# A chunked delta-rule scan on one core: 64x64 products spread over four parts of the matmul array, with new places for its steps

## The chip, the core and the metric

The kernel runs on one core of a Trainium2 chip. The core has TensorE (PE in the profile; PEld is its weight loading), VectorE (DVE), ScalarE (ACT), GpSimd (POOL) and SyncE (SP), each with an instruction stream of its own, held together by semaphores. Matmul results land in PSUM: 8 banks of 512 fp32 values for each of 128 partitions. The metric is the time of one execution on the device in microseconds.

## The reference

Two transformer blocks run one after the other, on 256 context rows and 256 image rows of width 1024. The first has two gated FFNs, window attention and a gated scan; the second has two layers, of which the first mixes latent attention with an RWKV-7 scan, and each ends in a mixture of experts. Everything is fp32. The change touches only the RWKV-7 scan: 8 heads of width 64, forward and backward, over context and then image rows:

```
def wkv7_scan(state0, r, w, k, v, a_vec, b_vec, reverse):
    def step(S, inp):
        r_t, w_t, k_t, v_t, a_t, b_t = inp
        sa = jnp.einsum('bhij,bhj->bhi', S, a_t)
        S = (S * w_t[:, :, None, :] + sa[..., None] * b_t[:, :, None, :]
             + v_t[..., None] * k_t[:, :, None, :])
        return S, jnp.einsum('bhij,bhj->bhi', S, r_t)
    s_fin, ys = lax.scan(step, state0, xs, reverse=reverse)
```

## The kernel before

Class `Rwkv` computes the scan in **units**. A unit is one chunk of 128 tokens (`step`, 4 of them), one direction `d` and one pair of heads `j`: 4 x 4 x 2 = 32 units. Within a unit the sequential recurrence becomes matrix work. Decay factors `EB` and `EI` (ACT, two exponentials of 128 columns) scale the inputs into `RA` and `KB` (DVE). The products of `KB` and `RA` are 64-row matmuls with 256 columns (keys `mm`), which DVE copies through a triangular mask into `MM` (`copy_predicated`, L173, 512 columns each). Then the unit needs the inverse of a unit triangular 128x128 matrix for each of two heads. It is built in levels (`LEVELS`, 64 down to 1, finest first): POOL cuts the level's masked part `ML` out of the compact copy `MC`; TensorE forms T = ML X (key `lev`), ACT copies it to `T1`, TensorE forms two products of `T1` and X (key `xx`: X and its transpose are both kept in `XX`), and DVE adds them to `XX`. There are four 64x64 blocks, two heads `hh` by two token halves `b`. A matmul whose inputs lie in partition half `b` and whose output goes to partition half `b` uses one quarter of the array: quarter (b, b). So before, the level products use two of the four quarters, (0, 0) and (1, 1). The last level joins the halves, in an off-diagonal quarter, two matmuls for each product; its second product is named by `rwXF` and `rwT` (or `nv`, which is `T1` of buffer set 3). Then come `wu0` (128 columns), `wu1` (inverse times `wu0`), `st` (state update) and `y` (output).

Each level has 12 matmuls of 64x64 (4 in `lev`, 8 in `xx`), the first level 4. An fp32 matmul stands as two MATMUL records in the trace. Buffer set 0 of the four sets is carved out of `rwa`, so its operands are all named `rwa`; for sets 1 to 3 the names are `rwXX`, `rwT`, `rwMM`, `rwWU` (this holds `MC` and `ML` first), `rwXF`, and so on.

The order of the instructions is made by `run`: time is cut into rounds, a new unit starts every `APART` = 5 rounds, and in each round every running unit, oldest first, issues what stands between two `yield`s of its generator (`unit_pe`, `unit_act`, `unit_dve`, `unit_pool`). Four or five units are in flight. A level's `lev` goes in one round and its `xx` in the next. So five rounds are one period, in which TensorE issues as much as one unit has. `Banks.take` gives PSUM banks in rotation, and the taker waits until the bank's last user is emptied (`free`). A unit takes 20 banks. At the ends of the scan other work lies beside it: `amid_pe` at the start, and `close_*` with `late_pe` from round 146.

## Time and profile before

| | us |
|---|---|
| median of 3 runs | 2538.71 |
| lowest, highest | 2531.82, 2540.67 |
| the profiled execution | 2542.52 |
| its span in the profile | 2540.7 |

The page counts TensorE as busy for 92% of the span, DVE for 69%, ACT for 41%, POOL for 13%. The span is one chain of stages: FFNs and mixers before about 1400 us, the RWKV-7 scan from about 1405 to 1757 us, then the experts, the second mixer and the second experts. In the scan almost no DMA runs. A record of a 64x64 matmul lasts some 0.22 us from its start to its modelled end, while the next one on the same quarter starts much earlier, so the busy share of TensorE says less than the distances between starts. In the timeline, "x8" merges eight records; the time shown runs from the first start to the last end.

### The profile page before, as it was taken

The page shows a single profiled execution, that of the slowest core. Times are in us where ns is not written, and L with a number is a line of the kernel's source. Part 1 is how long each engine was busy: PE and PEld are TensorE (multiplying, and loading weights), DVE is VectorE, ACT ScalarE, POOL GpSimd, SP SyncE. Part 2 cuts the span into 40 slices and gives each one's busy share as a digit, 9 for nine tenths or more (in the row PEclk, how much of TensorE's full clock was granted, in tenths as well). Part 3 has the DMA queues.
Part 4 walks back from the last instruction along what each step waited for, and adds up shares of the span by engine and source line. Part 5 has one row for each costly group of instructions (what it writes and reads, how often), then busy time and mean ns, then how long its engine had stood idle before and what let it go on. Part 6 is the DMA issues. An engine that isn't in the chain of part 4 may idle for free.

```text
span 2540.7 us, 38727 instructions
## 1 busy us (share of the span) xinstructions
PE 2341.8 (92%) x15014; PEld 1751.2 (69%) x15014; DVE 1744.4 (69%) x3348; ACT 1051.7 (41%) x2068; POOL 337.2 (13%) x534
## 2 busy tenths in 40 slices
PE   7999999799989799989999899989999998998997
PEld 3788887465788799944454677775676775667775
DVE  4875687677756687834758666665678885748995
ACT  4222212224231434423134344442477773446884
POOL 0111110010001011000200233331011210001210
PEclk9999999899999899989998999999899999999998
DMA  8566654242226478711111000000389982126995
GB/s 307 190 204 199 216 197 161 94 141 91 101 74 206 142 265 269 254 43 66 39 43 35 18 3 3 2 3 26 109 286 341 324 314 108 59 70 216 338 339 188
DMA packets 114919, 386.47 MB, mean 152 GB/s; under 512 B 20144, under 2 KB 22320, under 8 KB 114480
## 3 DMA queue, kind: packets, MB, share of 16 engines
q1 hardware_dynamic: 76496, 275.81, 31.2%
q0 software_dynamic: 34848, 95.47, 11.3%
q10 hardware_dynamic: 3392, 12.72, 1.3%
q8 instruction: 119, 1.95, 0.3%
q14 instruction: 64, 0.52, 0.1%
HBM read 389.16 MB, written 26.21 MB: 163 GB/s over the span
## 4 chain that ended last, share of the span: by engine, by line
PE 37%; DVE 13%; DMA 8%; ACT 5%; issue 3%; POOL 0%; DVEq 0%; ACTq 0%; SPq 0%; POOLq 0%
PE ps L144 35%; DMA RG<-in_w 5%; DVE moe0wl L153 2%; PE ps L147 2%; DVE moe1wl L153 2%; DMA AR<-in_a 2%; DVE rwMM L173 1%; DVE f2wl L153 1%; DVE acc L161 1%; ACT moe0wh L150 1%; DVE H L161 1%; ACT moe1wh L150 1%; DVE rwXF L153 1%; ACT rwWU L150 1%; DVE rwXX L153 0%
## 5 line engine op out<-in xcount | busy, mean ns | idle before, releaser
L144 PE MATMUL ps<-H,RG 128*128 128x256 f32 (+2 forms) x1088 | 359.4, 491 | 14.0 <-ACT H L150 14.0
L161 DVE SCALAR_TENSOR_TENSOR acc<-AR,cs,acc 128x512 f32<-128x512 f32 x420 | 295.5, 746 | 48.9 <-DMA AR<-in_a 46.7
L144 PEld LDWEIGHTS ps<-H,RG 128*128 128x128 f32 (+1 forms) x1088 | 206.1, 194 | 149.8 <-issue 132.5
L153 DVE TENSOR_TENSOR moe0wl<-RG,moe0wh 128x1024 fp32r<-128x1024 f32 x144 | 173.6, 1219 | 42.8 <-ACT moe0wh L150 33.1
L150 ACT ACTIVATE moe0wh<-RG 128x1024 fp32r<-128x1024 f32 x144 | 150.8, 1061 | 73.9 <-DMA RG<-in_w 44.5
L200 POOL DMA_DIRECT2D AR<-in_a x152 | 82.1, 540 | 698.8 <-DVE acc L161 512.5
L150 ACT ACTIVATE f1wh<-RG 128x1024 fp32r<-128x1024 f32 x66 | 69.7, 1060 | 230.0 <-PE ps L144 229.9
L153 DVE TENSOR_TENSOR moe1wl<-RG,moe1wh 128x1024 fp32r<-128x1024 f32 x120 | 144.2, 1219 | 23.9 <-ACT moe1wh L150 19.8
L144 PE MATMUL ps<-f1hh,f1wh 128*128 128x512 f32 x352 | 142.5, 405 | 4.8 <-DVE f1hl L153 4.8
L150 ACT ACTIVATE moe1wh<-RG 128x1024 fp32r<-128x1024 f32 x120 | 125.9, 1060 | 46.8 <-DMA RG<-in_w 28.4
L144 PE MATMUL ps<-f1hl,f1wh 128*128 128x512 f32 x352 | 140.8, 400 | 0.0
L144 PE MATMUL ps<-f1hh,f1wl 128*128 128x512 f32 x352 | 140.7, 400 | 0.0
L153 DVE TENSOR_TENSOR f1wl<-RG,f1wh 128x1024 fp32r<-128x1024 f32 x66 | 80.4, 1221 | 54.8 <-ACT f1wh L150 53.1
L144 PE MATMUL ps<-f2hh,f2wh 128*128 128x256 f32 x352 | 103.2, 293 | 9.7 <-DVE f2hl L153 5.0
L144 PE MATMUL ps<-f2hh,f2wl 128*128 128x256 f32 x352 | 101.5, 288 | 0.0
L144 PE MATMUL ps<-f2hl,f2wh 128*128 128x256 f32 x352 | 101.4, 288 | 0.0
L150 ACT ACTIVATE f2wh<-RG 128x1024 fp32r<-128x1024 f32 x66 | 68.5, 1055 | 47.9 <-PE ps L144 47.9
L144 PE MATMUL ps<-moe0wh,moe0xh 128*128 128x512 f32 x184 | 78.6, 427 | 9.4 <-DVE moe0wl L153 9.3
L153 DVE TENSOR_TENSOR rwXX<-rwXX,ps 128x256 f32<-128x256 f32 (+1 forms) x120 | 47.1, 393 | 58.1 <-PE ps L144 57.5
L144 PE MATMUL ps<-rwa 64*64 64x64 f32 (+3 forms) x1228 | 74.5, 236 | 12.1 <-DVE rwa L153 5.6
L153 DVE TENSOR_TENSOR f2wl<-RG,f2wh 128x1024 fp32r<-128x1024 f32 x66 | 80.3, 1219 | 7.8 <-ACT f2wh L150 7.7
L144 PEld LDWEIGHTS ps<-f1hh,f1wh 128*128 128x128 f32 x352 | 68.6, 195 | 20.4 <-DVE f1hl L153 6.2
(633 smaller groups left out, 5742.3 us busy)
## 6 DMA issues: line engine op xcount, KB each, us to landing
RG<-in_w SPq DMA_DIRECT2D x524, 512.0 KB
AR<-in_a POOLq DMA_DIRECT2D x152, 512.0 KB, 3.9
moe0back<-moe_outs ACTq DMA_DIRECT2D x4, 1024.0 KB, 8.0
CT<-in_consts ACTq DMA_DIRECT2D x1, 2562.0 KB, 14.9
X<-in_x ACTq DMA_DIRECT2D x1, 2048.0 KB, 11.5
moe_rows<-moe0ht POOLq DMA_DIRECT2D x4, 512.0 KB, 5.4
moe1back<-moe_outs ACTq DMA_DIRECT2D x2, 1024.0 KB, 5.8
X<-in_ctx ACTq DMA_DIRECT2D x1, 1024.0 KB, 5.8
```

The source lines that it names most:

```text
L144: return Silent() if self.e is None else self.e.matmul(out, lhs, rhs, start=start, stop=stop, skip_group_check=True)
L147: return Silent() if self.e is None else self.e.transpose(out, x, ident)
L150: return Silent() if self.e is None else self.e.activation(out, x, f, **k)
L153: return Silent() if self.e is None else self.e.tensor_tensor(out, a, b, op)
L161: return Silent() if self.e is None else self.e.scalar_tensor_tensor(out=out, in0=a, scalar=s, in1=b, op0=op0, op1=op1)
L173: return Silent() if self.e is None else self.e.copy_predicated(out, mask, data)
L200: return Silent() if self.e is None else self.e.dma_start(out, src)
```

## The change

- `Banks` can hand out a pair of neighbouring banks (`take_pair`), and all banks are one PSUM tensor, so that one instruction can read both. A taker of a pair waits for the last users of both banks.
- In a level the block of head `hh` is kept in the partition half `b ^ hh`. `lev` and the first part of `xx` now use all four quarters in rotation, one matmul each, into a pair of banks. The second part of `xx` (4 matmuls) stays in the two diagonal quarters.
- T1 is I + ML X: DVE adds the identity while it empties the pair (128 columns). The product with T1 then replaces the old sum, so nothing is added afterwards: DVE copies 64 columns of the result, ACT the other 192. At the last small level DVE copies 128 columns, and ACT writes `XF` in four copies of 64x64. At the first level ACT copies 128 columns in place of a DVE add, and POOL forms the two halves of 64 columns in place of a DVE add.
- The product `mm` comes in two halves, for `KB[0]` in round 2 and for `KB[1]` in round 3, each with a mask copy; the transposes `kbt` follow in round 4. `wu1` moves from round 18 to the last slot of round 19, `y` and `st` from round 19 to round 20. The output copy of `y` on DVE now comes a round after the state's update.
- A round has four slots, and each step names its round and slot through `clock`.
- The three small ACT instructions for the chunk's middle are taken out of the units; six of 16 columns before the scan (`middles_act`) replace them.
- POOL writes the identity into the first 128 columns of `MM` (a copy of 2 x 128 columns beside a memset of 2 x 384).
- A unit takes 34 banks: 13 pairs and 8 single ones. The number of matmuls in a unit stays the same (86, or 172 records).

The level part of the diff, cut to its core:

```diff
+    def take_pair(self, key):
+        self.n += self.n % len(self.tiles) == len(self.tiles) - 1
+        b = self.n % len(self.tiles)
+        self.n += 2
+        self.hold(key, [b, b + 1])
+        return self.tiles[b], self.tiles[b + 1]
...
-            for u in list(running):
-                if next(u, "over") == "over":
-                    running.remove(u)
+            for _ in range(self.SLOTS):
+                for u in list(running):
+                    if next(u, "over") == "over":
+                        running.remove(u)
...
+        yield from to(2, 2)
+        self.mm_pe(e, n, 0, KB, RA)
+        yield from to(3, 2)
+        self.mm_pe(e, n, 1, KB, RA)
+        yield from to(4, 2)
         ps = g.banks.take(("kbt", n))
...
+            r = 4 + 2 * i if i else 5
+            if i == 6:
+                yield from to(r, 0)
+                self.wu0_pe(e, n, RA, MM, state, v)
+            yield from to(r, 1)
             key = ("lev", n, i)
-            ps = g.banks.take(key)
+            ps = g.banks.take_pair(key) if li else g.banks.take(key)
...
+            if i == 0:
+                e.wait_ge(*S.pool.at(("x1", n, 0)))
+                for k, b in enumerate(both):
+                    for hh in range(2):
+                        ins = e.matmul(ps[1 - hh][both[k ^ hh], 0:64], XX[b, 2 + hh, :], self.IC[b, :], True, True)
+            elif li:
...
+                for k, b in enumerate(both):
+                    for hh in range(2):
+                        ins = e.matmul(ps[hh][both[k ^ hh], 0:64], ML[b, hh, :], XX[b, 1 - hh, :], True, True)
...
+                yield from to(r + 1, 1)
                 key = ("xx", n, i)
-                ps = g.banks.take(key)
+                ps = g.banks.take_pair(key) if li else g.banks.take(key)
...
                 if li:
...
+                    for k, b in enumerate(both):
+                        for hh in range(2):
+                            ins = e.matmul(ps[hh][both[k ^ hh], 0:64], XX[b, 2 + hh, :], T1[b, hh, :], True, True)
+                    ins.then_inc(*p.up(("x0", n, i)))
                     for hh in range(2):
                         for b in both:
-                            e.matmul(ps[b, 128 + hh * 64:192 + hh * 64], T1[b, hh, :], XX[b, 1, hh, :], True, True)
-                    for hh in range(2):
-                        for b in both:
-                            ins = e.matmul(ps[b, hh * 64:(hh + 1) * 64], XX[b, 1, hh, :], T1[b, hh, :], True, True)
+                            ins = e.matmul(other[b, 64 + 64 * hh:128 + 64 * hh], T1[b, hh, :], XX[b, 2 + hh, :], True, True)
...
+        yield from to(2, 1)
+        e.wait_ge(*S.act.at(("ei", n)))
+        e.tensor_tensor(KB[:, 0, :], self.BB[d][:, j, cc], EI[:, :], MUL).then_inc(*v.up(("kb", n, 0)))
...
+                e.tensor_tensor(T1[:, :, :], g.banks.pair(("lev", n, i))[:, :, 0:64], one, ADD).then_inc(*v.up(("t", n, i)))
...
+        yield from to(20, 0 if step < 3 else 3)
+        if step < 3:
...
+            yield from to(21, 0)
         y = self.YB[:, j, cc]
```

How the change moves instructions is best seen in the order on the engines. First, TensorE in the middle of a period, before: a level's `xx` of set 2, a `lev` of set 3, then the four products `mm` of the new unit (set 0) together, and its transposes right behind.

```order
L144 MATMUL ps6<-rwXX2,rwT12 64x64 [waits rw_act]
L144 MATMUL ps6<-rwXX2,rwT12 64x64 x3
L144 MATMUL ps6<-rwT12,rwXX2 64x64 x4
L144 MATMUL ps7<-rwXX3,rwWU3 64x64 [waits rw_pool,rw_dve]
L144 MATMUL ps7<-rwXX3,rwWU3 64x64 x3
L144 MATMUL ps0<-rwa 128x256 [waits rw_dve]
L144 MATMUL ps1<-rwa 128x256
L144 MATMUL ps0<-rwa 128x256
L144 MATMUL ps1<-rwa 128x256
L147 MATMUL ps2<-CT,rwa 128x128 x2
```

The same place in the changed kernel:

```order
L144 MATMUL ps<-rwXX2,rwWU2 64x64 [waits rw_act,rw_pool,rw_dve]
L144 MATMUL ps<-rwXX2,rwWU2 64x64 x3
L144 MATMUL ps<-nv,rwXX3 64x64 [waits rw_dve]
L144 MATMUL ps<-nv,rwXX3 64x64 x3
L144 MATMUL ps<-rwXX3,nv 64x64 x4
L144 MATMUL ps<-rwa 128x256 [waits rw_dve]
L144 MATMUL ps<-rwa 128x256
L144 MATMUL ps<-rwT12,rwXX2 64x64 x4
L144 MATMUL ps<-rwXX2,rwT12 64x64 x4
L144 MATMUL ps<-rwXX3,rwWU3 64x64 [waits rw_pool,rw_act]
L144 MATMUL ps<-rwXX3,rwWU3 64x64 x3
L144 MATMUL ps<-rwa 128x256 [waits rw_dve]
```

The products `mm` are now in two pieces with level products between them, and the first piece waits for DVE.

Second, TensorE where a unit ends (set 1) and the next one's levels begin, in the changed kernel: `y`'s last products, an `xx` of set 2, a `lev` of set 3, the first level of a younger unit (set 0), and `wu0` of set 2.

```order
L144 MATMUL ps<-rwMM1,rwvk 64x128 x2
L144 MATMUL ps<-rwMM1,rwWU1 64x128 x2
L144 MATMUL ps<-rwT12,rwXX2 64x64 [waits rw_dve]
L144 MATMUL ps<-rwT12,rwXX2 64x64 x3
L144 MATMUL ps<-rwXX2,rwT12 64x64 x4
L144 MATMUL ps<-rwXX3,rwWU3 64x64 [waits rw_pool,rw_act]
L144 MATMUL ps<-rwXX3,rwWU3 64x64 x3
L144 MATMUL ps<-rwa 64x64 [waits rw_pool,rw_dve]
L144 MATMUL ps<-rwa 64x64 x3
L144 MATMUL ps<-rwst,rwRA2 128x128
L144 MATMUL ps<-rwvk,rwMM2 128x64 x2
```

Before, this first level took a single bank. Now it takes a pair, and it waits for a count of DVE as well as for one of POOL. Its data come from POOL alone: the count is that of a bank's last user, which in the rotation is the `y` of the unit that ends here (the same in every period). Before, `wu1`, `st` and `y` stood at this place behind the transposes, and no level product waited for the output copy.

Third, VectorE at the same place. Before (the unit that ends is in set 3), from the mask copies on:

```order
L173 COPY_PREDICATED rwMM2<-CT,ps0 128x512 [waits rw_pool,rw_pe]
L173 COPY_PREDICATED rwMM2<-CT,ps1 128x512 [waits rw_pe]
L164 COPY rwk<-ps4 128x128 [waits rw_pe]
L153 TENSOR_TENSOR rwst<-rwst,ps3 64x64 x2
L158 TENSOR_SCALAR rwst<-rwst,rwEB3 128x128 [waits rw_dve]
L153 TENSOR_TENSOR rwXX1<-rwXX1,ps6 128x256 [waits rw_pe]
```

And in the changed kernel (the unit that ends is in set 1):

```order
L153 TENSOR_TENSOR rwst<-rwst,ps 64x64 [waits rw_pe]
L153 TENSOR_TENSOR rwst<-rwst,ps 64x64
L158 TENSOR_SCALAR rwst<-rwst,rwEB1 128x128 [waits rw_dve]
L164 COPY rwXX2<-ps 128x128 [waits rw_pe]
L153 TENSOR_TENSOR nv<-ps,rwa 128x128 [waits rw_pe]
L164 COPY rwk<-ps 128x128
```

The output copy (`rwk`) moved from ahead of the state's update to behind it, and behind the answers to the `xx` and the `lev` that TensorE issues after `y`.

## Rows read from the trace of the kernel before

**Rows 1.** The page, part 1: busy time, share of the span, instructions.

```profile
PE 2341.8 (92%) x15014; PEld 1751.2 (69%) x15014; DVE 1744.4 (69%) x3348; ACT 1051.7 (41%) x2068; POOL 337.2 (13%) x534
```

**Rows 2.** Busy times by stretch: length, then PE, PEld, DVE, ACT, POOL, clock, DMA.

```profile
1530.00:1585.00 55.00, 50.09 (x930) 42.24 (x924) 35.42 (x115) 22.26 (x91) 19.84 (x40) 1.00 0.01 2
```

**Rows 3.** Chain that ended last, 1568 to 1590: start, us, what; mask copies of successive units.

```profile
1568.25 1.34 DVE rwa L173 x2
...
1578.36 1.35 DVE rwMM L173 x2
...
1588.49 1.33 DVE rwMM L173 x2
```

**Rows 4.** Timeline of PE in one period: start, us, instruction, idle before.

```profile
1574.40 0.22 PE L144 MATMUL ps<-rwXF,rwT 64*64 64x64 f32 x1
1574.86 0.45 PE L144 MATMUL ps<-rwXX,rwWU 64*64 64x64 f32 x8 [0.24 <-DVE rwXX L153]
...
1576.33 0.45 PE L144 MATMUL ps<-rwXX,nv 64*64 64x64 f32 x8
1576.62 0.40 PE L144 MATMUL ps<-nv,rwXX 64*64 64x64 f32 x8
1576.85 0.40 PE L144 MATMUL ps<-rwa 64*64 64x64 f32 x8
1577.18 1.13 PE L144 MATMUL ps<-rwRA,rwXX 64*128 64x256 f32 x8
1578.24 0.44 PE L147 MATMUL ps<-CT,rwXX 128*128 128x128 f32 x2
...
1580.15 0.63 PE L144 MATMUL ps<-rwa 64*64 64x64 f32 x16
1581.01 0.45 PE L144 MATMUL ps<-rwXX,nv 64*64 64x64 f32 x8 [0.23 <-ACT nv L150]
...
1581.80 0.43 PE L144 MATMUL ps<-rwa,rwWU 64*64 64x64 f32 x8
1582.59 0.44 PE L144 MATMUL ps<-rwXX,rwMM 64*64 64x64 f32 x4 [0.36 <-DVE rwXF L153]
```

**Rows 5.** Timeline of PE: an off-diagonal product (rwXF) beside a diagonal one.

```profile
1644.95 0.23 PE L144 MATMUL ps<-rwXX,rwWU 64*64 64x64 f32 x2
1644.96 0.27 PE L144 MATMUL ps<-rwXF,rwT 64*64 64x64 f32 x1
1645.01 0.28 PE L144 MATMUL ps<-rwXX,rwWU 64*64 64x64 f32 x3
...
1645.13 0.22 PE L144 MATMUL ps<-rwXX,rwWU 64*64 64x64 f32 x1
1645.19 0.22 PE L144 MATMUL ps<-rwXF,rwT 64*64 64x64 f32 x1
```

**Rows 6.** Timeline of DVE in the same period.

```profile
1576.36 0.28 DVE L153 TENSOR_TENSOR rwRA<-abr,rwEB 128x128 f32<-128x128 f32 x1
1576.56 0.28 DVE L153 TENSOR_TENSOR rwXX<-rwbb,rwT 128x128 f32<-128x128 f32 x1
...
1577.29 0.41 DVE L153 TENSOR_TENSOR rwXX<-rwXX,ps 128x256 f32<-128x256 f32 x1
1578.34 1.36 DVE L173 COPY_PREDICATED rwMM<-CT,ps 128x512 f32<-128x512 uint32 x2 [0.64 <-PE ps L144]
...
1580.19 0.46 DVE L153 TENSOR_TENSOR rwst<-rwst,ps 64x64 f32<-64x64 f32 x2
```

**Rows 7.** Timeline of ACT in the same period.

```profile
1575.93 0.19 ACT L150 ACTIVATE rwEB<-H 128x1 f32<-128x1 f32 x1
...
1579.74 0.64 ACT L150 ACTIVATE rwWU<-rwMM 64x128 f32<-64x128 f32 x2 [2.17 <-DVE rwMM L173]
1580.40 0.38 ACT L150 ACTIVATE rwKBt<-ps 128x256 f32<-128x256 f32 x1
1580.68 0.27 ACT L150 ACTIVATE nv<-ps 128x128 f32<-128x128 f32 x1
```

More of the change, by code:

```diff
@@ L349, in __init__ @@
         self.CL, self.VL, self.ncst = CL, VL, ncst
-        self.banks = Banks([outer.enter_context(nc.psum_tensor(f"ps{i}", [P, 512], F32)) for i in range(8)])
+        self.banks = Banks(outer.enter_context(nc.psum_tensor("ps", [P, 8, 512], F32)))
         sb = self.sb
@@ L2668, in pool @@
             e.wait_ge(*o.now())
+        for d in range(2):
+            e.tensor_tensor(self.LC[d][:, 5, :], self.LC[d][:, 5, :], self.IC[:, :], ADD).then_inc(*o.up())
+            e.wait_ge(*o.now())
         for B in self.sets:
@@ L2692, in run, with clock, to @@
                 beside(e, r)
+    def clock(self):
+        at = [0]
+        def to(r, slot):
+            for _ in range(r * self.SLOTS + slot - at[0]):
+                at[0] += 1
+                yield
+        return to
     def last(self, j):
@@ L2787, in unit_pe @@
         src, dst = self.halves(d)
-        yield
-        yield
-        yield
-        got = []
-        for hh in range(2):
-            got.append(g.banks.take(("mm", n, hh)))
-            for tok in g.banks.free(("mm", n, hh)):
-                e.wait_ge(*tok)
-        e.wait_ge(*S.dve.at(("kb", n)))
-        for q in range(2):
-            for hh, b in enumerate(both):
-                ins = e.matmul(got[hh][:, q * 256:(q + 1) * 256], KB[b, q, :], RA[b, :], True, True)
-                if q:
-                    ins.then_inc(*p.up(("mm", n, hh)))
+        to = self.clock()
+        yield from to(2, 2)
[3 more added lines that the diff above has]
+        yield from to(4, 2)
         ps = g.banks.take(("kbt", n))
@@ L2836, in unit_pe @@
                 if li:
+                    other = ps[0]
+                    if li == 1:
+                        other, ps = g.banks.take(("xf", n)), ps[::-1]
+                        for tok in g.banks.free(("xf", n)):
+                            e.wait_ge(*tok)
+                    for k, b in enumerate(both):
+                        for hh in range(2):
+                            ins = e.matmul(ps[hh][both[k ^ hh], 0:64], XX[b, 2 + hh, :], T1[b, hh, :], True, True)
+                    ins.then_inc(*p.up(("x0", n, i)))
@@ L2845, in unit_pe @@
                         ins = e.matmul(ps[src, hh * 64:(hh + 1) * 64], T1[dst, hh, :], XF[dst, hh, dst], True, True)
[L2846 to L2847 removed]
+                ins.then_inc(*p.up(("x1", n, i)))
+        yield from to(19, 3)
         ps = g.banks.take(("wu1", n))
@@ L2855, in unit_pe @@
         ins.then_inc(*p.up(("wu1", n)))
-        yield
+        yield from to(20, 0)
         u = WU[:, 1, :]
-        e.wait_ge(*S.act.at(("wu1", n)))
+        out = g.banks.take(("y", n))
+        for tok in g.banks.free(("y", n)):
+            e.wait_ge(*tok)
+        e.matmul(out[:, 0:P], state, RA[:, P:2 * P], True, False)
         if step < 3:
@@ new lines, in unit_dve @@
+        yield from to(4, 0)
+        masks(1)
+        one = mid(self.IC[:, :], 2, 64)
+        for i, li in self.levels()[1:]:
+            if li:
+                yield from to(4 + 2 * i, 1)
+                e.wait_ge(*S.pe.at(("t", n, i)))
+                e.tensor_tensor(T1[:, :, :], g.banks.pair(("lev", n, i))[:, :, 0:64], one, ADD).then_inc(*v.up(("t", n, i)))
+                g.banks.done(("lev", n, i), v.now())
+                yield from to(5 + 2 * i, 1)
+                e.wait_ge(*S.pe.at(("x0", n, i)))
+                new = g.banks.pair(("xx", n, i))
+                if li > 1:
+                    e.tensor_copy(XX[:, 0, :], new[:, 1, 0:64]).then_inc(*v.up(("x0", n, i)))
+                    g.banks.done(("xx", n, i), v.now(), S.act.at(("x1", n, i)))
+                else:
+                    e.tensor_copy(XX[:, 0:2, :], new[:, :, 0:64]).then_inc(*v.up(("x0", n, i)))
+                    g.banks.done(("xx", n, i), v.now())
+            else:
+                yield from to(5 + 2 * i, 0)
+                e.wait_ge(*S.pe.at(("x1", n, i)))
+                e.tensor_copy(XF[src, :, dst], two(g.banks.of(("xx", n, i))[src, 0:128])).then_inc(*v.up(("xf", n)))
+                g.banks.done(("xx", n, i), v.now())
@@ new lines, in unit_dve @@
+        yield from to(20, 0 if step < 3 else 3)
+        if step < 3:
+            last = e0 + (P - 1 if d == 0 else 0)
+            e.wait_ge(*S.pe.at(("st", n)))
+            e.wait_ge(*S.pe.at(("y", n)))
+            e.wait_ge(*v.at(("ts", n)))
+            for lo in (0, 64):
+                q = slice(lo, lo + 64)
+                e.tensor_tensor(state[q, q], state[q, q], g.banks.of(("st", n))[q, lo:lo + 64], ADD).then_inc(*v.up())
+            g.banks.done(("st", n), v.now())
+            e.wait_ge(*v.now())
+            e.tensor_scalar(state, state, EB[:, last:last + 1], None, MUL).then_inc(*v.up())
+            v.note(("end", n))
+            yield from to(21, 0)
@@ L2997, in unit_dve @@
         g.banks.done(("y", n), v.now())
[L2998 to L3008 removed]
+        if step == 3:
+            v.note(("end", n))
     def unit_pool(self, e, n, step, d, j, B):
```

265 lines of the change are left out of this document (128 added, 137 removed).

## The prediction

> **What bounds the kernel now.** I read the page first: TensorE is busy for 92% of the span [rows 1]. Then the stretches: inside the scan TensorE works 50.1 of 55 us, DVE 35.4, ACT 22.3, POOL 19.8, at granted clock 1.00 and with a DMA share of 0.01 [rows 2]. So no transfer and no other engine fills the time. Then the chain of waits: the mask copies of successive units start at 1568.25, 1578.36 and 1588.49 [rows 3], a period of 10.12 us for each unit. 32 units start in the scan, so 31 periods lie between the first and the last.
>
> Then the timeline of TensorE in one period [rows 4], read by distances between starts. Eight records in the two diagonal quarters take 0.23 us: from 1576.62 to 1576.85. So a quarter takes a record each 0.058 us. A group that starts after idle time takes 0.05 more at its second record: four records in one quarter (1582.59, 0.44 long, of which 0.22 is the last record's own length) have starts 0.22 apart, 0.107 + 2 x 0.058. Where the tile shape changes, the distance to the next start is longer: the group at 1576.85 ends its starts at 1577.03, and 1577.18 comes 0.147 later instead of 0.058, so a change costs 0.09. The real waits are three in the period: 1580.57 (0.63 long from 1580.15, less 0.22) to 1581.01, beyond the pace 0.38; 1582.01 to 1582.59, 0.52; and 1574.40 to 1574.86, 0.40. Together 1.3 us. The rest, 8.8 us, is work at TensorE's pace.
>
> **What an answer costs** [rows 4, 6, 7]. DVE starts 0.26 us after the last start of a 64x64 group (1577.03 to 1577.29), and 0.41 after that of `mm` (1577.18 + 1.13, less the last record's 0.38, to 1578.34). TensorE starts 0.05 after the answering instruction ends (ACT 1580.68 + 0.27 = 1580.95, with rounding, to 1581.01). DVE instructions of 128 columns last 0.28 and start 0.20 apart (1576.36, 1576.56). A mask copy occupies 0.64 (1.36 for two, less 0.72). ACT: 128 columns 0.27, 256 columns 0.38.
>
> **Part one, the products.** The diagonal quarters bound the levels. Before, each of them has 2 matmuls at the first level and 6 at each of five levels: 32, of two records. Now it has 1 and 1 + 3 at each of five: 21. That removes 11 x 2 x 0.058 = 1.28 us for each unit, if the off-diagonal quarters run beside the diagonal ones. Rows 5 show three quarters at once: `rwXF` is an off-diagonal product; its four records (1644.96 to 1645.19) lie among eight diagonal ones (1644.95 to 1645.13), which keep their 0.18 from first to last start. Twelve records fit in 0.24 us, 0.022 each. The off-diagonal quarter there shares its inputs' half with one diagonal quarter and its outputs' half with the other. Four at once no row shows.
>
> `mm` in two pieces: one more change into and out of its shape, and one less between it and `kbt`: +0.09. A piece of two matmuls takes 0.32 (first records, with the start) + 0.30 to the next shape, twice: 1.25, where [rows 4] has 1577.18 to 1578.24, 1.06; in all +0.19. The work becomes about 8.8 - 1.28 + 0.19 = 7.7, and a little less where the first record's extra 0.05 goes: 7.55 in the walk below.
>
> **Part two, the waits.** I walk one period by the order and the prices above. A is the oldest unit in its levels, B and C are younger, N is the new one. Prices that no row has: DVE's copy of 64 columns, between 0.21 to 0.23 (two adds of 64x64 in 0.46) and 0.28: 0.22, occupying 0.17. ACT's copy of 192 columns, between 0.27 and 0.38: 0.33. ACT's 64x64 copies for `XF`, between 0.19 (one column) and 0.31: 0.22, and nothing waits for them soon. Zero is A's last level product.
> - B's `xx` runs beside it, 6 records to a diagonal quarter, last start 0.35. C's `lev` starts to 0.47. ACT answers in order: A's T1 at 0.48, `wu0` at 0.66, B's 192 columns from 0.83 to 1.16. A's `XF` product starts at 0.80 and B's `lev` at 1.21. The diagonal quarters stood idle for 0.68.
> - DVE has a queue here: C's T1 at 0.78, the two `RA`, `XF`, B's T1 at 1.59, C's copy at 1.79, and then `KB[0]` from 1.96 to 2.25. C's `xx` is issued from 1.38 to 1.67, and `mm` could start at 1.82, but waits for `KB[0]` to 2.30: 0.48.
> - From there TensorE never waits for long: B `xx` 2.94, C `lev` 3.34, second `mm` 3.55, B `lev` 4.18, C `xx` 4.35, transposes 4.79, `wu1` 5.28, the state products 5.72 (with 0.04 for `wu1`'s copy), `y` to 6.91, B `xx` 7.11, C `lev` 7.51. The mask copies (3.04 and 4.38 on DVE) cover nothing that TensorE needs sooner, since each answer has 0.8 us or more.
> - The first level of N could start at 7.63. It takes a bank that `y` held, and DVE's output copy stands behind C's T1: 7.57 + 0.26 = 7.83, copy from 8.04 to 8.33, TensorE at 8.38. Wait: 0.75.
> - `wu0` 8.64, the next last level 9.46.
>
> So the period is 9.46 us, with 1.9 us of waits where there were 1.3. The gain in work, 1.25, loses half to new waits: 0.66 us for each period.
>
> Of banks: a unit takes 34 where it took 20, so that eight are gone round in 2.2 us (9.46 x 8 / 34) instead of 4.0, and `y` holds one from 5.72 to 8.33. The Trainium skill says of this in "TensorEngine Tiling (Array Packing)", Gotcha 1: PSUM Pressure, that different row tiles have to write to different banks and so need more of them; my walk has it as the wait of 0.75, and without it the period would be 8.7.
>
> **Off the path.** POOL's memset and identity copy together cost between 0.95 (as now) and about 1.4; POOL would be busy for some 4 of 9.5 us, and each mask level is asked for a round earlier: nothing. DVE loses about 0.6 us in a period, ACT gains 1: both are under 7. Six ACT instructions of 16 columns before the scan, by the row of 0.19 [rows 7], cost at most 1.1 on the path and at least 0.5, as ACT starts overlap: 0.8. At the end of the scan five levels lose about 0.2 us each in latency, and `wu1` and `y` come a round or more later, in rounds that hold little; the closing of heads 2 now asks for an output of its own round, a stop of about 0.5. These cancel to within 1.5: zero.
>
> **The sum.** 31 x 0.66 = 20.5, less 0.8: 19.7 us. The profiled execution has 2542.52 (span 2540.7) and would come to 2522.8. It lies 3.8 above the median of the three timed runs, so that against the median the forecast is 2538.7 - 19.7 = **2519.0**.
>
> **The rivals.**
> 1. *The off-diagonal quarters do not run beside both diagonal ones, and it becomes slower.* Then a `lev` takes 0.23 and an `xx` 0.47 as now, 0.117 more in each of 11 groups, ten of them on the path, and the new waits stay: 9.46 + 1.17 = 10.63, or 31 x 0.51 + 0.8 = 16.6 more, 2555. It turns from gain to loss where more than 0.66 is lost, six of the groups. Against it: [rows 5] for three quarters. For it: no row for four.
> 2. *TensorE's issue is the limit, and nothing changes.* The longest dense stretch in rows, 8 records in 0.23, is 0.029 each, and only a stretch of twelve reaches 0.022 [rows 4, 5]; with 0.022 a `lev` takes 0.18 instead of 0.12 and the period is 9.8 (2530), with 0.029 it is rival 1. Halfway, at some 0.025, a `lev` takes 0.20 and an `xx` 0.40: 6 x 0.08 + 5 x 0.05 = 0.73, period 10.2, 2542. The Trainium skill has just such a rule in "TensorE: Matmul & The Clock Gate", section "Wait — 56ns, not 53.3ns?": starts never come closer than about 25 ns, however small the matmul. By that rule the result would be this rival's; pairs of starts 0.01 us apart in [rows 5] speak against it for different quarters.
> 3. *The waits come out smaller.* If the bank wait is hidden, 8.71 for the period: 2538.7 - 43.7 + 0.8 = 2496. Order and rotation speak against it, since the wait is there in each period. Without any wait (7.55) it would be 2460, which the answer times forbid.
> 4. *The waits grow instead*: DVE's queue before `KB[0]` holds seven instructions, and each 0.1 there moves the period by 0.1. At 10.0 the result is 2536, no change.
>
> **Chances.** Forecast (2507 to 2531): 0.52. Rival 3: 0.16. Rivals 2 and 4, no change: 0.19. Rival 1 and anything slower: 0.13. A measurement of this kernel can tell about 0.3%, 7.6 us, from no change. Faster by more: 0.52 x 0.96 + 0.16 = 0.66; within: 0.21; slower: 0.13. To leave out no more than 2 in 10 the range goes from 2496 (rival 3) to 2549, halfway into rival 1.
>
> **What would show it.** Mask copies of successive units 9.46 us apart, not 10.12. Eight records of a `lev` within some 0.12 to 0.18 us between first and last start; 0.23 would be rival 1. The first level waiting for DVE, some 0.7 us; the first piece of `mm` waiting for DVE's multiply, some 0.5; the `lev` after `rwXF` waiting for ACT. DVE busy a little less, ACT a little more in the scan, and every stage outside it as before. The prediction is wrong if periods are under 9 (waits overrated) or over 9.9 (products or queue underrated), or if another stage moves by more than 2 us.

## The result

The changed kernel takes 2569.27 us (median; 2554.74 to 2572.72), the kernel before beside it 2537.15 (2531.82 to 2540.67): a ratio of 1.0111, interval 1.0076 to 1.0145. It is 32 us slower by the medians, 28 by the ratio; the ratio rests on four executions of each kernel. The forecast was 2519.0, and 2569 is also outside its range. The profiled execution has 2572.72, its span 2570.9.

The page of the changed kernel, part 1, and the row of TensorE's granted clock from part 2:

```profile
PE 2337.3 (91%) x15014; PEld 1729.8 (67%) x15014; DVE 1726.1 (67%) x3380; ACT 1087.9 (42%) x2170; POOL 348.2 (14%) x600
...
PEclk9999999899999899999998989899999999998998
```

Against [rows 1] busy times hardly differ: 4.5 us less of PE, 18 less of DVE, 36 more of ACT. The row of the clock has an 8 in slices 24 and 26 (of 64.3 us each), which lie in the scan; before, no slice wholly within the scan has one. The windows say where to look. Length, then PE, PEld, DVE, ACT, POOL, granted clock, DMA share:

```profile
1530.00:1585.00 55.00, 45.04 (x826) 35.26 (x822) 28.77 (x107) 25.29 (x98) 18.61 (x44) 0.91 0.01 2
...
1640.00:1695.00 55.00, 46.38 (x768) 36.54 (x761) 26.68 (x97) 23.88 (x92) 17.75 (x42) 0.81 0.01 2
...
1582.00:1595.00 13.00, 10.12 (x226) 7.90 (x218) 7.95 (x31) 6.60 (x25) 4.75 (x11) 1.00 0.00 1
1570.00:1575.00 5.00, 4.60 (x63) 2.89 (x63) 3.08 (x12) 2.06 (x8) 1.15 (x3) 0.56 0.00 0
```

[Rows 2] had 930 PE records in 55 us at clock 1.00. Now there are 826 at 0.91, later 768 at 0.81. Two different things are in that: TensorE works 45 instead of 50 us of 55 (it stops more), and part of the time its clock is at the lower of its two levels, 1.2 GHz instead of 2.4. From 1570 to 1575 nearly all of the time is at it (0.56); from 1582 to 1595 none.

So the scan is read in two numbers for each kernel below: the period at full clock (the mean distance between first mask copies of successive units, over those periods of the fourth to the 27th that hold no slow clock), and how much of the time between the first unit's mask copy and the last's was at 1.2 GHz, summed over the clock's records in the trace. Before: period 10.11, none at 1.2 GHz, 318.7 us in all. Changed: period 10.40, 64.9 us at 1.2 GHz, 348.6 us. The 29.9 us between them are the loss; the stages before the scan start and end as before, those behind it only start later.

The 24 periods from the fourth to the 27th divide this loss. They take 242.8 us before and 269.7 in the changed kernel. Of the 26.9 between, 24 x (10.40 - 10.11) = 7 are the longer period at full clock. The other 20 go with the 51.2 us at 1.2 GHz that lie in these periods, 0.39 for each. The seven periods at the two ends hold the remaining 3. So most of the loss is the slow clock.

One period at full clock, TensorE. Start, us, instruction, idle before and what ended it:

```profile
1583.15 0.34 PE L144 MATMUL ps<-rwXX,rwWU 64*64 64x64 f32 x8
1583.28 0.33 PE L144 MATMUL ps<-nv,rwXX 64*64 64x64 f32 x8
1583.40 0.43 PE L144 MATMUL ps<-rwXX,nv 64*64 64x64 f32 x8
1584.47 0.70 PE L144 MATMUL ps<-rwa 64*128 64x256 f32 x4 [0.63 <-DVE rwa L153]
...
1589.15 0.39 PE L144 MATMUL ps<-rwMM,rwWU 128*64 128x128 f32 x4
1589.47 0.34 PE L144 MATMUL ps<-rwT,rwXX 64*64 64x64 f32 x8
...
1589.86 0.29 PE L144 MATMUL ps<-rwXX,rwWU 64*64 64x64 f32 x6
1591.34 0.34 PE L144 MATMUL ps<-rwa 64*64 64x64 f32 x8 [1.19 <-DVE rwk L153]
...
1592.95 0.32 PE L144 MATMUL ps<-rwa 64*64 64x64 f32 x4
1593.23 0.44 PE L144 MATMUL ps<-rwXF,rwT 64*64 64x64 f32 x4
1593.96 0.34 PE L144 MATMUL ps<-rwXX,rwWU 64*64 64x64 f32 x8 [0.28 <-POOL rwa L153]
```

Eight records of a `lev` or of the first part of `xx` last 0.34, less the last record's 0.22: 0.12 from first to last start, half of the 0.23 of [rows 4]. The four quarters run side by side in full. The three stops stand where the forecast has them, and each is longer: from 1583.61 (1583.40 + 0.43 - 0.22) to 1584.47, 0.86; from 1589.93 to 1591.34, 1.41; from 1593.05 to 1593.96, 0.91, in which only XF's product runs.

DVE in the longest of these stops (in every other `step` the output copy is an add, as here):

```profile
1589.65 0.47 DVE L153 TENSOR_TENSOR rwst<-rwst,ps 64x64 f32<-64x64 f32 x2 [1.86 <-PE ps L144]
1590.16 0.29 DVE L158 TENSOR_SCALAR rwst<-rwst,rwEB 128x128 f32<-128x128 f32 x1
1590.48 0.29 DVE L164 COPY rwXX<-ps 128x128 f32<-128x128 f32 x1
1590.68 0.28 DVE L153 TENSOR_TENSOR nv<-ps,rwa 128x128 f32<-128x128 f32 x1
1591.00 0.29 DVE L153 TENSOR_TENSOR rwk<-rwk,ps 128x128 f32<-128x128 f32 x1
```

The state's adds start at 1589.65, 0.11 after the modelled end of the last product of `y` (1589.15, 0.39 long), though their own product `st` came before `y`'s other products; DVE had been idle for 1.86 us. Behind them in the queue stand the scaling, the two answers, and the output copy (`rwk`), which ends at 1591.29. TensorE starts 0.05 later.

### The profile page after: what moved, and what is told of

It is laid out like the page before. It is cut to its first block, busy times and chain, and to the rows that moved or that the text cites. A ratio compares the mean times of both kernels' runs of the same rounds, so it can differ in the third digit from the quotient of the medians.

```text
span 2570.9 us, 38923 instructions
## 1 busy us (share of the span) xinstructions
PE 2337.3 (91%) x15014; PEld 1729.8 (67%) x15014; DVE 1726.1 (67%) x3380; ACT 1087.9 (42%) x2170; POOL 348.2 (14%) x600
## 4 chain that ended last, share of the span: by engine, by line
PE 34%; DVE 15%; DMA 10%; ACT 4%; issue 3%; POOL 0%; DVEq 0%; ACTq 0%; SPq 0%; POOLq 0%
PE ps L144 32%; DMA RG<-in_w 7%; DVE moe0wl L153 2%; DMA AR<-in_a 2%; PE ps L147 2%; DVE moe1wl L153 2%; DVE f2wl L153 1%; DVE acc L161 1%; ACT moe1wh L150 1%; ACT moe0wh L150 1%; DVE H L161 1%; DVE rwT L153 0%; DMA moe0back<-moe_outs 0%; DVE rwst L153 0%; DVE rwXX L164 0%
## 5 line engine op out<-in xcount | busy, mean ns | idle before, releaser
L153 DVE TENSOR_TENSOR moe1wl<-RG,moe1wh 128x1024 fp32r<-128x1024 f32 x120 | 144.4, 1219 | 25.4 <-ACT moe1wh L150 23.8
L150 ACT ACTIVATE rwa<-ps 128x192 f32<-128x192 f32 (+5 forms) x119 | 38.5, 324 | 103.5 <-PE ps L144 90.2
```

The costliest lines, as they stand in the source:

```text
L150: return Silent() if self.e is None else self.e.activation(out, x, f, **k)
L153: return Silent() if self.e is None else self.e.tensor_tensor(out, a, b, op)
```

## The experiments

Where not said otherwise the kernels are the changed one with the edit shown. The ratio is to the kernel before, run on the same chip (its medians there: 2537.1 to 2541.9).

| kernel | median us | ratio, interval | scan us | of it at 1.2 GHz | full-clock period |
|---|---|---|---|---|---|
| before | 2537.15 | | 318.7 | 0 | 10.11 |
| changed | 2569.27 | 1.0111 (1.0076 to 1.0145) | 348.6 | 64.9 | 10.40 |
| e1 | 2588.18 | 1.0191 (1.0157 to 1.0225) | 372.8 | 153.6 | none |
| e2 | 2548.32 | 1.0044 (1.0025 to 1.0064) | 324.9 | 37.5 | 9.96 |
| e3 | 2555.98 | 1.0073 (1.0050 to 1.0096) | 338.5 | 34.1 | 10.41 |
| e4 | 2564.45 | 1.0096 (1.0072 to 1.0121) | 345.4 | 92.2 | 10.23 |
| e5 | 2535.76 | 0.9989 (0.9970 to 1.0007) | 315.1 | 30.7 | 9.62 |
| e6 | 2525.45 | 0.9955 (0.9930 to 0.9980) | 307.5 | 27.3 | 9.36 |
| e7 | 2522.99 | 0.9933 (0.9910 to 0.9955) | 300.8 | 23.9 | 9.09 |
| e8 | 2586.64 | 1.0190 (1.0163 to 1.0218) | 360.7 | 44.4 | 10.80 |
| e9 | 2536.82 | 0.9987 (0.9970 to 1.0005) | 313.0 | 4.2 | 9.76 |
| e10 | 2545.09 | 1.0017 (1.0000 to 1.0034) | 327.2 | 45.9 | 9.91 |
| e11 | 2529.09 | 0.9966 (0.9950 to 0.9983) | 310.1 | 25.4 | 9.57 |

Scan times and periods are of one profiled execution each. In e10 and e11 27.3 us of the slow clock are one stretch at the scan's end; e11 has none from the fourth to the 27th period.

### e2: the state's adds wait for their own products only

The adds change `ST` in place, so they have to wait until TensorE has read the state for `y`. The changed kernel makes them wait for all of `y`; its first product alone reads the state.

```diff
-        e.matmul(out[:, 0:P], state, RA[:, P:2 * P], True, False)
+        e.matmul(out[:, 0:P], state, RA[:, P:2 * P], True, False).then_inc(*p.up(("ys", n)))
...
-            e.wait_ge(*S.pe.at(("y", n)))
+            e.wait_ge(*S.pe.at(("ys", n)))
```

> The changed kernel, but DVE's update of the state waits only for the product of y that reads the state, not for the last product of y. This is the one wait that the prediction's walk left out: it had the update at 6.6 us of the period, and the trace has it about 0.55 us later. If that is the term, the stop before the first level falls from 1.40 to about 0.85 us and the full-clock period from 10.4 to 9.85. Theory A: 31 x 0.5 = 16 us less, and part of the clock comes back: 2535 to 2553. Theory B: 2553. Theory C: no change, 2569.

The period falls by 0.44, the time by 21 us, within the expected 2535 to 2553. TensorE at the same place in e2:

```profile
1594.21 0.29 PE L144 MATMUL ps<-rwXX,rwWU 64*64 64x64 f32 x6
1595.24 0.34 PE L144 MATMUL ps<-rwa,rwXX 64*64 64x64 f32 x8 [0.74 <-DVE rwk L153]
```

From 1594.28 to 1595.24 are 0.96 us instead of 1.41: that is the 0.45. The wait for all of `y` is shown to be a cause. The clock too falls less often (37.5 us instead of 64.9).

### e3: the stop is filled with idle matmuls

```diff
+            if i == 0 and 6 <= n < 28:
+                idle = g.banks.of(("wu1", n - 3))
+                for _ in range(4):
+                    e.matmul(idle[:, 0:P], g.C("ident"), g.C("ident"), True, True)
             ps = g.banks.take_pair(key) if li else g.banks.take(key)
```

> The changed kernel plus four 128x128 matmuls of the identity in 22 of the 32 periods, in the stop of 1.40 us before the first level, into a bank whose content nobody needs any more. Their eight records fill about 1.1 us of the stop at the full clock. No wait is taken away, so the full-clock period stays at 10.4. Theory A (the clock falls because TensorE stands still in the stops): the clock in the scan rises from 0.91 towards 1.00 and up to two thirds to all of the 27 us that it costs come back: 2545 to 2552, although the kernel does more work. Theory B (the clock falls because of the products in four quarters): 2569 or a little more.

The groups of PE from 1475 to 1695, by form: busy us, mean ns, idle time before and who ended it. First the changed kernel, then e3 (the filler, and the same first level):

```profile
L144 PE MATMUL ps<-rwa,rwXX 64*64 64x64 f32 x120 | 5.2, 245 | 18.5 <-DVE rwk L164 11.3 <-DVE rwk L153 7.1
```

```profile
L144 PE MATMUL ps<-CT 128*128 128x128 f32 x167 | 24.2, 288 | 0.0
...
L144 PE MATMUL ps<-rwa,rwXX 64*64 64x64 f32 x120 | 5.2, 242 | 1.6 <-DVE rwk L164 1.0
```

The first level still waits for the same copy of DVE, and the full-clock period stays at 10.41 (10.40 before), but TensorE is not idle meanwhile. It does more work and the kernel is faster: 13 us by the medians, 10 by the scan, with 34.1 us at 1.2 GHz instead of 64.9. So each us at 1.2 GHz that went brought 10.1 / 30.8 = 0.33 us, near the 0.39 within the changed kernel. The expectation had 2545 to 2552.

By the times alone this is not clear of noise, as the intervals of the two ratios overlap. The executions of the changed kernel itself bear it out: three have a mean granted clock of 0.952 to 0.954 over the whole execution and take 2568.83 to 2572.72 us; the fourth has 0.961 and takes 2554.74, with the same instructions. With e8 below, the slow clock is shown to be a loss of its own, and stops are shown to bring it on.

### e8: the kernel before, with a stop put in

Three dependent multiplies of DVE stand ahead of one answer in 24 periods. Products, banks and order of TensorE are those of the kernel before.

```diff
+            if i == 3 and 4 <= n < 28:
+                for _ in range(3):
+                    e.wait_ge(*v.now())
+                    e.tensor_scalar(self.KKn[:, j, :], self.KKn[:, j, :], 1.0, None, MUL).then_inc(*v.up())
+                e.wait_ge(*v.now())
```

> The kernel before, products in two quarters, with a stop put in: in 24 of 32 periods DVE multiplies 512 columns by one, three times in sequence, ahead of one of its answers (about 2 us), so that TensorE stands still for about 1.5 us more in each of these periods. No product and no wait changes otherwise. Theory A (stops alone let the clock fall): the clock in the scan falls as in the changed kernel, to about 0.9, and the time is 24 x 1.5 = 36 us plus some 20 to 40 more: 2595 to 2615. Theory B (the clock falls because of four quarters): the clock stays at 1.00 in the scan and only the 36 us show: 2573.

TensorE around one such stop in e8, and the window of 220 us of e8, then of the kernel before:

```profile
1590.08 0.22 PE L144 MATMUL ps<-rwXF,rwT 64*64 64x64 f32 x1
1591.79 0.45 PE L144 MATMUL ps<-rwXX,rwWU 64*64 64x64 f32 x8 [1.49 <-DVE rwXX L153]
```

```profile
1475.00:1695.00 220.00, 186.83 (x3198) 156.70 (x3194) 165.35 (x452) 79.29 (x315) 74.38 (x130) 0.94 0.01 2
1475.00:1695.00 220.00, 201.33 (x3678) 169.38 (x3677) 142.20 (x454) 89.82 (x366) 74.58 (x151) 1.00 0.01 2
```

A stop of 1.71 us in each of 24 periods takes the mean granted clock of this stretch from 1.00 to 0.94, with products in two quarters only. So stops bring the clock down without four-quarter products. That these do not do it without long stops, e11 shows below. The added stops alone explain less than half of the 46 us. Two of the 13 full-clock periods of the table hold no added stop; the eleven that do take 10.92 on average, 0.81 more than before, some 19 us over 24 periods. The time, 2587, lies between the two that were expected (2595 to 2615, and 2573 with a full clock).

### e1 and e4: the output copy ahead of the state's update

e1 puts DVE's output copy in front of the adds and the scaling, so that the bank is free early; e4 also has ACT's `EI` and DVE's multiply for `KB[0]` a slot or more earlier.

```diff
+        y = self.YB[:, j, cc]
+        e.wait_ge(*S.pe.at(("y", n)))
+        if step % 2 == 0:
+            e.tensor_copy(y, g.banks.of(("y", n))[:, 0:P]).then_inc(*v.up(("out", n)))
...
         if step < 3:
...
-            e.wait_ge(*S.pe.at(("y", n)))
...
-            yield from to(21, 0)
...
```

And in e4 besides (with ACT's `EI` right behind `EB` in round 1):

```diff
-        yield from to(2, 1)
+        yield from to(2, 0)
         e.wait_ge(*S.act.at(("ei", n)))
         e.tensor_tensor(KB[:, 0, :], self.BB[d][:, j, cc], EI[:, :], MUL).then_inc(*v.up(("kb", n, 0)))
```

> The changed kernel, but on DVE the output copy of y stands ahead of the state's update, right behind y, as in the kernel before. In the changed kernel's trace a full-clock period is about 10.4 us and TensorE stands still for 1.40 us (1589.94 to 1591.34) before the first level, for a bank that y held. Theory A (the new waits cost twice, in themselves and because the clock falls in the idle time): the copy can end at about 1589.9, so the 1.4 us go, some 0.2 come back elsewhere, the period is 9.2 us, the clock stays at 1.00 in the scan, and the time is 31 x 0.9 = 28 us under before: 2510. Theory B (the wait goes, but the clock falls in any case, because TensorE gets through its 64x64 products in less time): the same 1.2 us a period are won against the changed kernel, but the clock still costs some 27 us: about 2532. Theory C (another wait behind it takes its place): about 2560.

> e1 plus the second stop: EI's exponential and the multiply that makes KB[0] are moved ahead of the answers of round 2 (a round's slot earlier on ACT and DVE), so that the first piece of mm finds its input ready. In the changed kernel's trace this piece starts 0.85 us after the level product before it, 0.15 of which is the change of shape. Theory A: 0.4 to 0.6 us less for each period than e1, full clock, 2495. Theory B: as e1 less 5 to 15 us. Theory C (the answers in round 2 come later by what the multiply takes, and the level product behind XF waits longer instead): as e1.

e1 is the slowest kernel of all. The stop before the first level is down to 0.42 us, but TensorE has one before `wu0`, and its scan is at 1.2 GHz for 153.6 us. In e4 the same stop is there, and 92.2 us are at 1.2 GHz. TensorE, DVE and POOL in e1 at this place:

```profile
1585.19 0.34 PE L144 MATMUL ps<-rwa,rwXX 64*64 64x64 f32 x8 [0.19 <-DVE rwst L153]
1586.66 0.68 PE L144 MATMUL ps<-rwst,rwRA 128*128 128x128 f32 x2 [1.12 <-DVE rwXX L164]
```

```profile
1584.63 0.46 DVE L153 TENSOR_TENSOR rwst<-rwst,ps 64x64 f32<-64x64 f32 x2
1585.13 1.16 DVE L158 TENSOR_SCALAR rwst<-rwst,rwa 128x128 f32<-128x128 f32 x1
1586.32 0.29 DVE L164 COPY rwXX<-ps 128x128 f32<-128x128 f32 x1
```

```profile
1585.12 0.41 POOL L153 TENSOR_TENSOR rwWU<-rwWU,rwa 128x128 f32<-128x128 f32 x1 [1.42 <-PE ps L144]
1585.47 0.74 POOL L179 MEMSET rwa<- 128x768 f32 x1
1586.15 0.40 POOL L164 COPY rwa<-CT 128x256 f32<-128x256 f32 x1
```

From the first level's last start (1585.31) to `wu0` TensorE stops for 1.35 us. It waits for a copy of DVE that stands behind the scaling. The scaling lasts 1.16 us, where the changed kernel's lasts 0.29 (1590.16). It starts 0.01 after POOL's multiply and ends 0.08 after the end of POOL's memset. The expectations had not thought of that, and all of them missed (2510, 2532 or 2560 for e1; 2495, or at most 15 us under e1, for e4).

### e10 and e11: e1 and e4 with POOL's memset later

```diff
-        yield from to(1, 1)
+        yield from to(2, 2)
         if n >= self.NS:
             e.wait_ge(*S.pe.at(("y", n - self.NS)))
         e.memset(MM[:, :, P:4 * P], 0.0).then_inc(*o.up())
```

> e1_output_first with one step of POOL moved: the memset of MM and the identity copy go from round 1, slot 1, to round 2, slot 2. In the trace of e1 all 24 of DVE's scalings of the state (TENSOR_SCALAR, 128x128, SBUF to SBUF) last 1.16 to 1.20 us, against 0.29 in the changed kernel; each starts 0.01 us after a POOL multiply and ends 0.08 after the end of POOL's memset (example: 1585.13 to 1586.29; POOL multiply 1585.12, memset 1585.47 to 1586.21). Theory A (DVE's scaling is held up by POOL's chain, and that is why e1 was slow): now only the multiply of 0.41 stands there, the scaling lasts 0.3 to 0.7, the stop of PE before `wu0` falls from about 1.1 to 0.3 to 0.7 us, the granted clock in the scan rises from 0.77 to over 0.93, and the time comes to 2535 to 2555. Theory B (the 1.2 us have another cause, in the order on DVE itself): scaling still 1.2, time within 0.5% of e1's 2588. Rival C (the memset now collides with another instruction of DVE, the factor multiplies or the mask copy): the scaling is short, but another DVE row is long by 0.4 to 0.9, and the time stays over 2560.

> e4_output_first_factor_early (2564.5, ratio 1.0096) with the same move of POOL's memset and identity copy to round 2, slot 2. Theory A (the scaling is held up by POOL's chain): the scaling lasts 0.3 to 0.7 instead of 1.16 to 1.20, full-clock periods fall from 10.0 to 10.3 to about 9.1 to 9.6, little of the scan is at half clock, and the time comes near that of e6 and e7: 2523 to 2540. Theory B: within 0.5% of e4. It should lie under e10 by some 0.4 us in each period, as e5 lay under e2.

The scalings by the line's view: count, then duration in ns, least, median and most; of e1, then of e10:

```profile
L158 DVE TENSOR_SCALAR rwst<-rwst,rwEB x18: 1197/1201/1203, 1452.9 to 1722.0; 128x128 f32<-128x128 f32 x18
L158 DVE TENSOR_SCALAR rwst<-rwst,rwa x6: 1156/1159/1162, 1440.1 to 1684.1; 128x128 f32<-128x128 f32 x6
```

```profile
L158 DVE TENSOR_SCALAR rwst<-rwst,rwEB x18: 286/526/529, 1446.0 to 1671.5; 128x128 f32<-128x128 f32 x18
```

With only POOL's multiply beside it the scaling lasts 0.48 (multiply of 0.41) or 0.53 (multiply of 0.46). The stop before `wu0`, 1.34 to 1.39 in e1 and e4, is 0.67 to 0.71 in e10 and e11 (from 1475 to 1650 us). e1's 2588 become 2545, e4's 2564 become 2529, both as expected. So POOL's memset right behind its multiply, beside DVE's scaling, is shown to have made e1 slow. The Trainium skill has the rule in "SBUF — State Buffer", section "Who interferes with whom": a DVE `tensor_scalar` that reads and writes SBUF in a two-port mode needs the port pair that GpSimd uses, whoever issues first keeps it for the whole instruction, and the other blocks. The traces agree on the blocking. By their rows (e1 and e10) the scaling did not get in between POOL's multiply and the memset behind it (1.16), though it did where nothing stood behind the multiply (0.53).

e11 also has the products in four quarters, with TensorE busy for 88% of this stretch and at full clock throughout:

```profile
1475.00:1680.00 205.00, 180.60 (x3667) 140.85 (x3661) 134.28 (x471) 111.56 (x428) 81.83 (x194) 1.00 0.01 3
```

So the four-quarter products by themselves do not bring the clock down.

### e5, e6 and e7: repairs one by one

e5 is e2 with the early `KB[0]` of e4. e6 is e2 with the output copy between the adds and the scaling, and e7 is e6 with the early `KB[0]`.

```diff
-            e.wait_ge(*v.now())
-            e.tensor_scalar(state, state, EB[:, last:last + 1], None, MUL).then_inc(*v.up())
-            v.note(("end", n))
-            yield from to(21, 0)
...
+        summed = v.now()
...
+        if step < 3:
+            e.wait_ge(*summed)
+            e.tensor_scalar(state, state, EB[:, last:last + 1], None, MUL).then_inc(*v.up())
```

> e2 (state update waits for one product only) plus the early multiply of e4 (EI and KB[0] ahead of the answers of round 2). e2's full-clock period is 9.80 to 10.02 us; its first piece of mm starts 0.85 us after the level product before it. If the queue of answers on DVE before KB[0] is the second term, 0.4 to 0.5 us go: a full-clock period of 9.4 to 9.5, and 13 us less than e2's 2548: 2535. Rival (the clock falls more, since the work is denser between the stops that are left): 2550 or more, with more time at half clock than e2's 37 us.

> e2, and the output copy of y stands on DVE between the two adds to the state and the state's scaling: so the bank of y is emptied some 0.3 us after y ends, the adds stand in time that DVE had free, and the copies behind them (which held up wu0 in e1) come no later than in e2. Both terms at the unit's end are undone then. The stop before the first level (0.96 us in e2, 1.40 in the changed kernel) goes, and the stop of 1.39 us before wu0 that took its place in e1 does not come. Full-clock period 9.0 to 9.2. If the clock falls because of single long stops: full clock nearly throughout, 2537 - 30 = 2507 to 2515. If it falls because TensorE gets through its products in less time whatever the stops are: 60 us or more at half clock, 2525 to 2545.

> e6 plus the early multiply: all stops that the prediction's walk names but the one behind XF are undone. Full-clock period 8.6 to 8.8. With the full clock: 2537 - 42 = 2495. If the clock falls with density of products alone: as e6 or 2530.

DVE in e6, with the copy at its new place, and the first level on TensorE:

```profile
1587.02 0.47 DVE L153 TENSOR_TENSOR rwst<-rwst,ps 64x64 f32<-64x64 f32 x2 [1.18 <-PE ps L144]
1587.62 0.29 DVE L164 COPY rwk<-ps 128x128 f32<-128x128 f32 x1
1587.94 0.29 DVE L158 TENSOR_SCALAR rwst<-rwst,rwa 128x128 f32<-128x128 f32 x1
```

```profile
1587.97 0.34 PE L144 MATMUL ps<-rwa,rwXX 64*64 64x64 f32 x8
```

The first level (1587.97) follows the `lev` of 1587.90 without a stop. The period goes from e2's 9.96 to 9.36. The early factor is worth 0.34 (e5 against e2) and 0.27 (e7 against e6). e7 is the fastest of all: 0.67% under the kernel before, with 17.9 us less in the scan, which is its whole gain. e5 is not told apart from the kernel before; its time was expected (2535). e6 and e7 were hoped to reach periods of 9.0 to 9.2 and 8.6 to 8.8 and came to 9.36 and 9.09; of that difference no run shows the cause.

### e9: e7 with the products in two quarters

```diff
-                for k, b in enumerate(both):
-                    for hh in range(2):
-                        ins = e.matmul(ps[hh][both[k ^ hh], 0:64], ML[b, hh, :], XX[b, 1 - hh, :], True, True)
+                for hh in range(2):
+                    for b in both:
+                        ins = e.matmul(ps[hh][b, 0:64], ML[b, hh, :], XX[b, 1 - hh, :], True, True)
```

(and so for the first level and the first part of `xx`; the blocks of the two heads are mixed up by it, so that e9 computes something else than the reference, and only its time is read)

> This is e7_output_between_factor_early (2523.0, full-clock period 8.99) with the level products sent back to the two diagonal quarters: first level, `lev` and the first part of `xx` issue the same matmuls, but each with its output in the partition half of its inputs. Banks, copies, waits and the order of everything else stay. The blocks of the two heads are thus mixed up and the output is not the reference's; the scan's time alone is read. Theory A (the products are worth what the prediction took): a group of eight records takes 0.23 from first to last start where it takes 0.13, some 0.117 more in each of 11 groups of a unit, ten of them on the path: period 8.99 + 1.17 = 10.16, 36 us more in 31 periods, about 2559. Rival B (half of it lies beside stops that are there in any case: the stops before `lev` after XF and before the mask copies' readers shrink): period 9.5 to 9.7, 2540 to 2546. Rival C (TensorE is not the bound any more once the quarters share the work): period under 9.2, under 2531. If the longer groups fill what were stops, the granted clock should also stay at 1.00; if stops of over 1 us appear, it will fall for stretches.

The same group of eight in e7, then in e9, and the windows of both:

```profile
1591.89 0.34 PE L144 MATMUL ps<-rwXX,rwWU 64*64 64x64 f32 x8
```

```profile
1475.00:1695.00 220.00, 196.69 (x3918) 154.72 (x3917) 138.22 (x504) 119.12 (x462) 87.76 (x209) 0.95 0.01 3
```

```profile
1592.58 0.40 PE L144 MATMUL ps<-rwXX,rwWU 64*64 64x64 f32 x8
```

```profile
1475.00:1695.00 220.00, 208.14 (x3822) 170.90 (x3822) 137.49 (x491) 115.64 (x450) 86.05 (x203) 1.00 0.01 3
```

The eight take 0.18 in e9 (0.40 less 0.22; 0.23 with the step at a group's start) and 0.12 in e7. Full-clock periods are 9.76 and 9.09: four quarters are worth 0.67 us of the 1.17 that they take off TensorE's work on the path. The longer groups fill part of the stops: TensorE works 208 of 220 us, not 197, and its clock stays at 1.00, where e7 has 0.95. So with the same instructions and waits otherwise the products bring 12 to 14 us, not 36. This was rival B of the expectation, a little under its 2540 to 2546.

## Why the prediction was wrong

**The products, right in size.** Step one took 0.117 us off each group of eight and assumed that the off-diagonal quarters run beside both diagonal ones, which no row had shown. The rows of the changed kernel have it: 0.12 for eight records. Rival 1 did not happen. Rival 2 (issue as the limit) did not either: eight starts in 0.12 are one each 0.017 us, under the 0.022 of its first end. The Trainium skill's rule, in "TensorE: Matmul & The Clock Gate", section "Wait — 56ns, not 53.3ns?", that starts never come closer than some 25 ns, does not hold here for matmuls in different quarters: by it, as an estimate, eight records would need at least 7 x 0.025 = 0.175, and the traces have 0.12.

**The walk of one period, wrong by 0.94 us (10.40 instead of 9.46).** All three stops stand at the places and behind the engines that the walk names, and all were sized too small:
- The bank wait before the first level: 0.75 forecast, 1.41 less one step of 0.06 = 1.35 measured. The step that failed is the place of the state's adds on DVE. The walk left them where `st` lets them start; in the diff they wait for the whole of `y`. e2 takes that wait away and 0.44 us with it. The quoted order of the changed kernel shows the adds with a wait for TensorE, but not for which product: that stands only in the code. The rest of this stop is the output copy's place behind them, which the walk had seen: moving it (e6) takes 0.60 more off the period.
- The stop before the first piece of `mm`: 0.48 forecast; 0.86 less the 0.15 of a change of shape = 0.71 measured. The queue of seven on DVE was seen, and its end came 0.23 later. An earlier factor gets back 0.27 to 0.34 (e5, e7).
- The stop behind `rwXF`: 0.68 forecast, 0.91 less 0.06 = 0.85 measured.

The excesses are 0.60, 0.23 and 0.17, together 1.00, against the 0.94 of the period. Of the first, e2 traces 0.44 to its cause; where its other 0.16 comes from, and why the other two stops came out longer, was not tested. Over the 24 periods from the fourth to the 27th the 0.94 make some 23 us of the 50 by which the forecast missed in the scan (348.6 against 318.7 - 20.5 = 298.2).

**The clock, a term put at nothing.** The forecast priced everything at the granted clock of [rows 2], 1.00, as if it belonged to the stage. It changes with the stops of TensorE. With stops of 1.41, 0.86 and 0.91 in each period, 64.9 us of the scan are at 1.2 GHz, 51.2 of them in the same 24 periods, where they cost 20 us. The seven periods at the ends hold the other 7 to 8 us of the miss, 13.6 us of slow clock among them. By this division the kernel without the slow clock would be some 7 us slower in these 24 periods, not 27. e3 shows it from one side (stop filled, more work, less time), e8 from the other (stop put into the kernel before, clock falls). What combination of stops brings it down is open. In e8 1.71 us once a period do; e1, with 1.34 to 1.39 before `wu0`, has more than twice the slow clock of the changed kernel with its 1.41; in e9, where TensorE works 95% of the time, it stays up; in e7 it falls now and then (23.9 us, much of it at the two ends of the scan).

**Rival 3** (waits smaller, period 8.7, 2496) is what e7 comes near with two of the three places repaired: 9.09 and 2523. Of the gain of 1.02 in its period (10.11 - 9.09) the products hold 0.67 and the rest of the edits (T1 with the identity in it, no adds of `XX`, the moved steps, as e7 has them) 0.35. The time of the forecast, 2519, was nearly reached by this design, but not with this order of DVE's instructions.

**Rival 4** named DVE's queue before `KB[0]` and the direction, at 10.0 for no change; the period came to 10.4. That queue is 0.23 of the excess; the larger part stood in the queue at the unit's end. What it lacked was the clock, which makes a kernel with a period just above the old one lose 1%. A slower kernel had a chance of 0.13, and for another reason (rival 1).

**The banks.** The prediction says that matmuls with inputs in different partition halves have to write to different banks. The kernel before does not bear this out for the two diagonal quarters: they read different halves and write one bank, eight records in 0.23 us [rows 4]. Whether two quarters with the same output half could share a bank, so that no pair is needed, no run here tried.

**Off the path, right.** Stages outside the scan moved by nothing that can be told, ACT gained 36 us and DVE lost 18, as said (1 and 0.6 in each period). At the start of the scan the changed kernel has a period of 12.9 where the kernel before has 10.5, and every version with the new order has 12.7 to 12.9 there; the prediction had only looked at the end. That costs 2.4 us, and its cause was not tested.

## What to carry to other kernels

When TensorE's work is cut, first list for each later answer what its instruction really waits for (which product, not which engine) and what stands in front of it in the queue; a wait for a later product than needed cost 21 us here (e2), and all four quarters brought 12 to 14 (e9). Price a kernel with longer stops at a lower clock, and try filling a stop with idle matmuls before judging it: e3 was 10 to 13 us faster with more work. And an instruction moved on DVE has to be laid beside POOL's rows as well as TensorE's.

## What was not expected of the hardware

- The granted clock of TensorE falls to 1.2 GHz for stretches when it stops for 1.4 to 1.7 us once in a period of about 10 us, though it works 82 to 85% of the time: 0.90 on average in the changed kernel from 1475 to 1695, 0.94 in e8, against 1.00 in e9 at 95% and 1.00 in e11 at 88% (1475 to 1680), where no two starts of TensorE lie more than 0.84 us apart. Each us at 1.2 GHz cost 0.39 us in the changed kernel.
- Four 64x64 quarters take eight fp32 records in 0.12 us, and records of two independent groups lie between each other at a group's end, 0.01 us apart.
- A DVE scaling of 128x128 from SBUF to SBUF, 0.29 us alone, lasted 1.16 to 1.20 in 24 of 24 cases in which POOL's multiply started 0.01 us before it and the memset stood right behind that (e1), and 0.48 to 0.53 with the multiply alone (e10, 23 of 24; the 24th started 0.27 before the multiply and lasted 0.29).
